# Turning the query/key chunks of an mLSTM mixer by VectorE blocks and ScalarE copies in place of TensorE transposes, with a new timetable for the mixer head

## The chip, the core and the metric

The kernel runs on one core of a Trainium2 chip. The metric is the device time of one execution in microseconds. Before the change it is 2407.74 us, the median of 3 runs (2407.58 to 2408.61).

## The reference, cut to what matters

The program computes two blocks in a row over 256 rows of width 2048, all in float32: a first block (windowed attention and a gated feed-forward layer), and a second one whose first layer is an mLSTM mixer and whose second layer attends in a band. The change is in the mixer, and there in what happens to one head:

```python
def mlstm_mixer(h, w_in, conv_w, conv_b, gate_b, g_head, w_out):
    proj = h @ w_in                       # query/key, value, o, z: 512 columns a head each
    qk = jax.nn.silu(causal_conv(proj[..., :A_V0], conv_w, conv_b))   # 4 taps over the rows
    v, o, z = proj[..., A_V0:A_O0], proj[..., A_O0:A_Z0], proj[..., A_Z0:A_G0]
    ...
    ht = mlstm_chunkwise(heads(q), heads(k), heads(v), li, lf)
    ht = rmsnorm(ht, g_head)
    y = jax.nn.sigmoid(o) * ht * jax.nn.silu(z)
    return y @ w_out

def causal_conv(u, w, b):                 # out[s] = b + sum_j w[j] * u[s - 3 + j]
    ...
```

The kernel works on a head as plain causal attention over the 256 rows: scores of queries and keys, times a decay, divided by a sum. Queries and keys come out of the projection with rows on partitions. The convolution runs over rows, so they are turned first: channels on partitions, rows along the free axis.

## The kernel before, in words

Weights come in tiles of 256x512 (a **slot**, 512 KB). ScalarE copies a tile to `WH` in fp32r (its upper part, L1563), VectorE subtracts that from the tile and leaves the rest in `WL` (L2206), and TensorE multiplies three times for each row block and each half of the tile (L1171: upper by upper, L1172: weight rest by upper, L1173: weight upper by activation rest): 12 matmuls of 512 columns per slot. There are four `WH`/`WL` buffers (`NH`), and ScalarE and VectorE stand `LOOK` = 3 slots ahead of TensorE: at the point of their programs where TensorE starts slot g, they make slot g+3, whose buffer comes free when TensorE ends slot g-1. TensorE waits at the start of each slot for both halves of its tile. VectorE also reduces streamed tiles of other weight matrices (L2187, the "modulation" tiles) woven in among the weight tiles, about one to three slots.

Eight slots with one accumulator pair are a **chunk**. A mixer head has four chunks (query/key, value, o, z); after heads 3 and 7 an output projection follows. The rest of a head's work is written as tasks (`mix`, one each for TensorE, ScalarE and VectorE) that are moved on by one step at each **tick**, and there are two ticks to a slot. `yield` ends a step, `ticks(n)` lets n ticks pass. `mix` starts when chunk 0 of its head is complete; its tick 0 comes in the first slot of chunk 1, tick 32 in the first slot of chunk 3, and the next head's tick 0 is this head's tick 64. So the tick numbers are a timetable, written by hand, and every engine's queue is fixed in that order: an instruction that waits holds up all that stands behind it on its engine, the weight tiles included.

Before the change a head goes like this. Tick 0: ScalarE (L1417) and VectorE (L1973) copy the two row blocks of the query/key chunk from PSUM to `QK`. Ticks 4 and 7: TensorE turns them, four 128x128 transposes by `four_turns` (L809) each time, into a PSUM bank. Ticks 5, 6, 8 and 9: VectorE runs one `conv` each (a TENSOR_SCALAR, L1980, and three SCALAR_TENSOR_TENSOR, L1983, each waiting for the one before). Tick 10: TensorE builds the decay (L995 to L998), ScalarE takes the sigmoid of the result (L1422) and exponentials (L1427, L1428), VectorE multiplies (L2002, queries and keys are ready, `qm`). Tick 16: scores on TensorE (L1004, L1005), their product with the decay on VectorE (L2009, `pm`). Tick 17: values copied (L1433 on ScalarE, L2014 on VectorE). Ticks 22 to 24: denominator and numerators (L1015 to L1025). Ticks 48 and 49: o, z and the numerators are multiplied (L2046 to L2051).

From tick 50 the head's product `G1` is turned in a second way, without TensorE: `blocks_T` (L1645) transposes 32x32 blocks on VectorE into `TQ`, 128x512 at a time, and `quadrants` (L1229) has ScalarE put the blocks in place, 16 small copies from `TQ` to `MT`, two per tick. Then ScalarE (L1243) and VectorE (L1660) make the two parts of the output projection's operand from `MT`. The feed-forward layer uses the same two helpers.

Of the kernel before, what the change touches and what calls it, by code (L numbers as in the profile page):

```python
# [43 lines left out]
TQ_FFN, TQ_MIX, TQ_KEYS = 0, 11, 19  # L44

MV = {k: i + 1 for i, k in enumerate("qk cva cvb qm pm vv den q2 nv0 nv1 z0 y0 z1 y1".split())}
MA = {k: i + 1 for i, k in enumerate("qk sg ee vv sn0 sn1 o0 o1 z".split())}
# [512 lines left out]
def build(nc, A, out):  # L560
    ctx = ExitStack()
    with ctx:
# [203 lines left out]
        def tensor_program(e):  # L766
# [163 lines left out]
            def gates(_):  # L930
                b, full = take("gate")
                w.wait_ge(s_gact, 1)
                w.wait_ge(s_gate, 1)
                for k in range(8):
                    w.wait_ge(s_xt, 16 + (POS[4 + k // 2] if k < 4 else POS[8 + k]))
                    for kt in (2 * k, 2 * k + 1):
                        o, a = b[0:16, 0:256], XTH[:, kt]
                        e.matmul(o, WGH[:, kt], a, start=(kt == 0), stop=False)
                        e.matmul(o, WGL[:, kt], a, start=False, stop=False)
                        i = e.matmul(o, WGH[:, kt], XTL[:, kt], start=False, stop=(kt == 15))  # L940
                    if k < 7:
                        yield from ticks(1 if k < 4 else 2)
                i.then_inc(full, 1)
                yield
                give("gate", s_gact, 2)
                yield
                b, full = take("gate_t")
                w.wait_ge(s_gact, 2)
                for t in range(2):
                    i = e.transpose(b[:, 16 * t:16 * t + 16], GS[:, 128 * t:128 * t + 128], ident[0:16, 0:16])  # L950
                i.then_inc(full, 1)
                yield
                give("gate_t", s_gate, 2)
                yield from ticks(2)
                b, full = take("gate_sum")
                w.wait_ge(s_gate, 4)
                w.wait_ge(s_nsel, 4)
                e.matmul(b[:, 0:8], Ut, glf[:, 0], start=True, stop=True)
                e.matmul(b[:, 8:16], onesf, glf[:, 0], start=True, stop=False)
                e.matmul(b[:, 8:16], Ut, glf[:, 1], start=False, stop=True).then_inc(full, 1)  # L960
                yield
                give("gate_sum", s_gate, 5)
                yield
                b, full = take("gate_c")
                w.wait_ge(s_gate, 6)
                for t in range(2):
                    i = e.transpose(b[0:8, 128 * t:128 * t + 128], gc[:, t], ident[:])
                i.then_inc(full, 1)
                give("gate_c", s_gate, 7)
                yield from ticks(4)  # L970
                b, full = take("gate_m")
                w.wait_ge(s_gate, 8)
                for t in range(2):
                    i = e.transpose(b[:, 8 * t:8 * t + 8], MM[:, 128 * t:128 * t + 128], ident[0:8, 0:8])
                i.then_inc(full, 1)
                give("gate_m", s_gate, 9)
                yield

            def mix(h, ends, free):
# [3 lines left out]
                yield from ticks(4)  # L983
                for half in range(2):
                    b, full = take(("qkT", h, half))
                    w.wait_ge(s_mixa, ata("qk"))
                    w.wait_ge(s_mix, at("qk"))
                    four_turns(b, lambda j, t: QK[:, t, 128 * (2 * half + j):128 * (2 * half + j) + 128], full)
                    yield from ticks(2)
                    give(("qkT", h, half), s_mix, at("cva" if half == 0 else "cvb"))  # L990
                    yield
# [7 lines left out]
                give(("decay", h), s_mixa, ata("ee"))  # L999
                yield from ticks(6)  # L1000
# [7 lines left out]
                yield  # L1008
                gfree[ends[1][0]] = [(s_mixa, ata("vv")), (s_mix, at("vv"))]
                yield from ticks(5)  # L1010
                b, full = take(("den", h))
                w.wait_ge(s_mix, at("vv"))
# [16 lines left out]
                yield from ticks(6)  # L1029
                gfree[ends[2][0]] = [(s_mixa, ata("o0")), (s_mixa, ata("o1"))]  # L1030
                yield from ticks(16)
# [156 lines left out]
        def scalar_program(e):  # L1188
# [209 lines left out]
            def gates(_):  # L1398
                yield from ticks(11)
                b = full("gate")  # L1400
                e.activation(GS, b[0:16, 0:256], ACT.Copy).then_inc(s_gact, 1)
                yield from ticks(2)
                w.wait_ge(s_gate, 3)
                e.activation(gt2, gt, ACT.Exp).then_inc(s_gact, 1)
                w.wait_ge(s_gact, 3)
                e.activation(gt, gt2, ACT.Ln, bias=onesf[:, 0:1]).then_inc(s_gact, 1)
                yield from ticks(9)
                w.wait_ge(s_gate, 9)
                e.activation(thr, gt2, ACT.Exp, scale=-1.0).then_inc(s_gact, 1)
                yield  # L1410

            def mix(h, ends, free):
                at = lambda k, hh=h: NMV * hh + MV[k]
                w.wait_ge(s_unit, ends[0][1])
                if h:
                    w.wait_ge(*filled(("qkT", h - 1, 1)))
                e.activation(QK[:, 0], Gb[ends[0][0]][0][:, :], ACT.Copy).then_inc(s_mixa, 1)  # L1417
                yield from ticks(10)
                w.wait_ge(s_mix, at("cvb"))
                if h:  # L1420
                    w.wait_ge(s_mix, at("y1", h - 1))
                e.activation(SG, CV.rearrange("p a b -> p (a b)"), ACT.Sigmoid).then_inc(s_mixa, 1)  # L1422
# [6 lines left out]
                yield from ticks(7)  # L1429
                w.wait_ge(s_unit, ends[1][1])  # L1430
                if h:
                    w.wait_ge(s_mix, at("y1", h - 1))
                e.activation(VV[:, 0], Gb[ends[1][0]][0][:, :], ACT.Copy).then_inc(s_mixa, 1)  # L1433
                yield from ticks(6)
# [167 lines left out]
        def vector_program(e):  # L1602
# [335 lines left out]
            def gates(_):  # L1938
# [17 lines left out]
                yield from ticks(2)  # L1956
# [9 lines left out]
            def mix(h, ends, free):  # L1966
# [23 lines left out]
                yield from ticks(5)  # L1990
# [7 lines left out]
                yield  # L1998
# [5 lines left out]
                yield from ticks(6)  # L2004
# [20 lines left out]
                yield from ticks(3)  # L2025
# [15 lines left out]
                yield from ticks(22)  # L2041
# [12 lines left out]
                w.wait_ge(s_mt, MT_MIX + h)  # L2054
# [433 lines left out]
```

## Time and profile before

| what | value |
|---|---|
| median of 3 runs | 2407.74 us |
| the profiled execution, its own time | 2407.68 us |
| its span, first to last instruction | 2405.9 us |
| TensorE matmuls busy | 2389.5 us, 99% of the span |
| VectorE busy | 1746.5 us, 73% |
| ScalarE busy | 1312.5 us, 55% |
| granted TensorE clock | 0.999 of full speed |

Busy time is the union of an engine's instructions. Matmuls are pipelined and their ends are modelled: two matmuls of the stream start 0.23 us apart while each is shown as 0.39 us long. So a pause of TensorE shorter than about 0.16 us shows only in the starts, and the starts are what is read here. Idle time is given with the instruction that ended it. "x4" in a timeline merges four instructions of one kind in a row.

### The profile page before, as it was taken

How to read it: one execution, taken by the hardware profiler on the slowest of the kernel's cores; microseconds unless marked ns; L12 is line 12 of the kernel's file. 1: busy time of each engine (PE TensorE's matmuls, PEld its weight loads, DVE VectorE, ACT ScalarE, POOL GpSimd, SP SyncE). 2: the span in 40 equal slices, each digit the busy share in tenths (PEclk: the TensorE clock that was granted, in tenths of full speed). 3: DMA queues.
4: the chain of work that ended last, by engine and by line, in shares of the span. 5: the costliest groups of instructions: out<-in, count | busy, mean ns of one | idle time of the engine just before them, and what ended most of it. 6: DMA issues, size and time to landing. Idle time of an engine off the chain costs nothing.

```text
span 2405.9 us, 30632 instructions
## 1 busy us (share of the span) xinstructions
PE 2389.5 (99%) x11049; PEld 1948.7 (81%) x11049; DVE 1746.5 (73%) x2436; ACT 1312.5 (55%) x1911; POOL 45.1 (2%) x65
## 2 busy tenths in 40 slices
PE   9999999999999999999999999999999999999998
PEld 7777888888888888778888888888888778888887
DVE  8885778677787776668778677677776676666665
ACT  6665465545553555555545544545455576655553
POOL 1100000000000000000000000000000000000000
PEclk9999999999999999999999999999999999999999
DMA  8445889788889897477777787777777457776654
GB/s 297 145 132 173 271 291 309 256 303 303 284 314 307 289 318 229 158 229 241 239 235 234 243 271 242 238 235 236 240 240 241 154 186 267 249 242 213 227 192 139
DMA packets 161831, 578.14 MB, mean 240 GB/s; under 512 B 18289, under 2 KB 20593, under 8 KB 161681
## 3 DMA queue, kind: packets, MB, share of 16 engines
q1 hardware_dynamic: 160432, 572.64, 71.4%
q0 software_dynamic: 1104, 3.28, 0.4%
q8 instruction: 90, 1.47, 0.3%
q14 instruction: 61, 0.49, 0.1%
q10 hardware_dynamic: 144, 0.26, 0.0%
HBM read 574.01 MB, written 2.10 MB: 239 GB/s over the span
## 4 chain that ended last, share of the span: by engine, by line
PE 94%; DVE 2%; ACT 2%; DMA 1%; issue 1%; POOL 0%; SPq 0%; DVEq 0%; ACTq 0%
PE PS L1171 30%; PE PS L1173 30%; PE PS L1172 30%; DVE WL L2206 1%; ACT WH L1563 1%; PE PS L914 1%; DMA X<-in_x 0%; PE PS L809 0%; PE PS L882 0%; DVE X L2173 0%; PE PS L1004 0%; PE PS L1072 0%; PE PS L1024 0%; PE PS L1025 0%; PE PS L1021 0%
## 5 line engine op out<-in xcount | busy, mean ns | idle before, releaser
L2206 DVE TENSOR_TENSOR WL<-W,WH 128x1024 fp32r<-128x1024 f32 x814 | 988.5, 1221 | 509.9 <-ACT WH L1563 503.9
L1563 ACT ACTIVATE WH<-W 128x1024 fp32r<-128x1024 f32 x814 | 855.1, 1058 | 723.6 <-PE PS L1173 681.0
L1171 PE MATMUL PS<-WH,XTH 128*128 128x512 f32 x2144 | 853.7, 398 | 2.8 <-DVE XTL L1718 1.2
L1173 PE MATMUL PS<-WH,XTL 128*128 128x512 f32 x2144 | 835.7, 390 | 0.0
L1172 PE MATMUL PS<-WL,XTH 128*128 128x512 f32 x2144 | 835.1, 389 | 0.0
L1171 PEld LDWEIGHTS PS<-WH,XTH 128*128 128x128 f32 x2144 | 402.7, 188 | 93.7 <-issue 11.4
L1173 PEld LDWEIGHTS PS<-WH,XTL 128*128 128x128 f32 x2144 | 402.5, 188 | 85.4
L1172 PEld LDWEIGHTS PS<-WL,XTH 128*128 128x128 f32 x2144 | 402.9, 188 | 83.8 <-issue 3.8
L1171 PE MATMUL PS<-WH,YTH 128*128 128x512 f32 x1120 | 440.2, 393 | 3.5 <-DVE WL L2206 2.4
L1173 PE MATMUL PS<-WH,YTL 128*128 128x512 f32 x1120 | 436.2, 389 | 0.0
L1172 PE MATMUL PS<-WL,YTH 128*128 128x512 f32 x1120 | 436.1, 389 | 0.0
L1171 PEld LDWEIGHTS PS<-WH,YTH 128*128 128x128 f32 x1120 | 210.3, 188 | 53.4 <-issue 9.0
L1173 PEld LDWEIGHTS PS<-WH,YTL 128*128 128x128 f32 x1120 | 210.3, 188 | 44.2
L1172 PEld LDWEIGHTS PS<-WL,YTH 128*128 128x128 f32 x1120 | 210.4, 188 | 42.3
L1229 ACT ACTIVATE MT<-TQ 32x256 f32<-32x256 f32 x304 | 126.3, 415 | 72.1 <-DVE TQ L1645 67.9
L2187 DVE CUSTOM_DVE_ANT_0 W<-W,acc,cols 128x1024 f32<-128x1024 f32 x96 | 122.6, 1277 | 0.8 <-ACT ZG L1551 0.8
L2187 DVE CUSTOM_DVE_ANT_0 W<-W,ZG,mods 128x1024 f32<-128x1024 f32 x96 | 122.7, 1278 | 0.0
L2241 DVE SCALAR_TENSOR_TENSOR acc<-W,SC,acc 128x512 f32<-128x512 f32 x64 | 48.1, 752 | 2.3
L1983 DVE SCALAR_TENSOR_TENSOR AR<-PS,cols,AR 128x255 f32<-128x255 f32 (+2 forms) x96 | 46.2, 482 | 3.4
L2238 DVE SCALAR_TENSOR_TENSOR acc<-W,SC,acc 128x512 f32<-128x512 f32 x56 | 41.7, 745 | 0.0
L1507 ACT ACTIVATE AR<-AR,st 128x128 f32<-128x128 f32 (+1 forms) x32 | 14.3, 449 | 44.4 <-DVE st L2110 44.4
L1645 DVE STREAM_TRANSPOSE TQ<-AR 128x512 f32<-128x512 f32 x46 | 31.6, 700 | 0.7
(286 smaller groups left out, 1192.6 us busy)
## 6 DMA issues: line engine op xcount, KB each, us to landing
W<-in_vec SPq DMA_DIRECT2D x192, 512.0 KB, 4.5
W<-in_avoz SPq DMA_DIRECT2D x192, 512.0 KB, 4.5
W<-in_wg SPq DMA_DIRECT2D x88, 512.0 KB, 5.1
W<-in_wu SPq DMA_DIRECT2D x88, 512.0 KB, 4.9
W<-in_wd SPq DMA_DIRECT2D x88, 512.0 KB, 4.9
W<-in_gate SPq DMA_DIRECT2D x64, 512.0 KB, 4.6
W<-in_aqk SPq DMA_DIRECT2D x64, 512.0 KB, 4.7
W<-in_aout SPq DMA_DIRECT2D x64, 512.0 KB, 4.4
```

The source lines that it names most:

```text
L914: i = e.matmul(b[64 * a:64 * a + 64, 0:m], V1[:, k, 64 * g:64 * g + 64], PT[P % 2][a][:, m * k:m * k + m], start=(k == 0), stop=(k == t))
L1171: e.matmul(p, x, WH[:, g % NH, j], start=first, stop=False)
L1172: e.matmul(p, x, WL[:, g % NH, j], start=False, stop=False)
L1173: i = e.matmul(p, y, WH[:, g % NH, j], start=False, stop=last)
L1229: i = e.activation(o, TQ[a].rearrange("p t (j b r) -> p t j b r", j=4, b=4)[:, :, :, b], ACT.Copy)
L1563: e.activation(WH[:, n % NH], W[:, i % NW], ACT.Copy).then_inc(s_hi, 1)
L1645: i = e.transpose(TQ[:, t], src[:, t])
L1983: i = e.scalar_tensor_tensor(out=o[:, s:256], in0=u[:, 0:256 - s], scalar=wt[3 - s], in1=o[:, s:256], op0=ALU.mult, op1=ALU.add)
L2187: e.tensor_tensor_reduce(W[:, s].rearrange("p k n -> p (k n)"), W[:, s].rearrange("p k n -> p (k n)"), SCR[h], 1.0, dst if h else cols[:, ...
L2206: e.tensor_tensor(l, src, h.bitcast(F32), ALU.subtract).then_inc(s_lo, 1)
L2238: step(e.scalar_tensor_tensor(out=a, in0=W[:, s, 0], scalar=SC[:, 2 * k:2 * k + 1], in1=a, op0=ALU.mult, op1=ALU.add))
L2241: e.scalar_tensor_tensor(out=a, in0=W[:, s, 1], scalar=SC[:, 2 * k + 1:2 * k + 2], in1=a, op0=ALU.mult, op1=ALU.add).then_inc(s_ada, 1)
```

## The change

The queries and keys of a head are now turned as `G1` is. At ticks 1 and 2 VectorE transposes the blocks of `QK` into `TQ`, at ticks 3 to 10 ScalarE copies the 16 quadrants to `MT`, and the convolutions read `MT` in SBUF at ticks 11, 12, 14 and 15. The two `four_turns` of each head leave TensorE's program, 64 transposes in all, and so do their two PSUM banks. `MT` and `TQ` are counted twice per head (`MT_MIX + 2 * h + 1` and `+ 2`). What follows is moved: values are copied at ticks 17 (ScalarE) and 18 (VectorE), the sigmoid and the exponentials come at tick 20 behind them, `qm` at tick 20, scores at tick 26, `pm` at tick 27, denominator at tick 33, numerators at 34 and 35, o at tick 37. The decay stays at TensorE's tick 10; z and the turn of `G1` stay at ticks 48 to 60. In the task `gates`, which runs beside head 0, two steps come two ticks later.

```diff
 MT_FFN, MT_MIX = 0, 11
-TQ_FFN, TQ_MIX, TQ_KEYS = 0, 11, 19
-
-MV = {k: i + 1 for i, k in enumerate("qk cva cvb qm pm vv den q2 nv0 nv1 z0 y0 z1 y1".split())}
-MA = {k: i + 1 for i, k in enumerate("qk sg ee vv sn0 sn1 o0 o1 z".split())}
+TQ_FFN, TQ_MIX, TQ_KEYS = 0, 11, 27
+
+MV = {k: i + 1 for i, k in enumerate("qk cva cvb vv qm pm den q2 nv0 nv1 z0 y0 z1 y1".split())}
+MA = {k: i + 1 for i, k in enumerate("qk vv sg ee sn0 sn1 o0 o1 z".split())}
 NMV, NMA = len(MV), len(MA)
...
     gfree[ends[0][0]] = [(s_mixa, ata("qk")), (s_mix, at("qk"))]
-    yield from ticks(4)
-    for half in range(2):
-        b, full = take(("qkT", h, half))
-        w.wait_ge(s_mixa, ata("qk"))
-        w.wait_ge(s_mix, at("qk"))
-        four_turns(b, lambda j, t: QK[:, t, 128 * (2 * half + j):128 * (2 * half + j) + 128], full)
-        yield from ticks(2)
-        give(("qkT", h, half), s_mix, at("cva" if half == 0 else "cvb"))
-        yield
+    yield from ticks(10)
     b, full = take(("decay", h))
...
     give(("decay", h), s_mixa, ata("ee"))
+    yield from ticks(10)
+    gfree[ends[1][0]] = [(s_mixa, ata("vv")), (s_mix, at("vv"))]
     yield from ticks(6)
...
     give(("qk", h), s_mix, at("pm"))
-    yield
-    gfree[ends[1][0]] = [(s_mixa, ata("vv")), (s_mix, at("vv"))]
-    yield from ticks(5)
+    yield from ticks(7)
     b, full = take(("den", h))
-    w.wait_ge(s_mix, at("vv"))
+    w.wait_ge(s_mix, at("pm"))
     w.wait_ge(s_mixa, ata("vv"))
...
     give(("num", h, 1), s_mix, at("nv1"))
-    yield from ticks(6)
+    yield
     gfree[ends[2][0]] = [(s_mixa, ata("o0")), (s_mixa, ata("o1"))]
-    yield from ticks(16)
+    yield from ticks(10)
     gfree[ends[3][0]] = [(s_mix, at("z0")), (s_mix, at("z1"))]
...
     if h:
-        w.wait_ge(*filled(("qkT", h - 1, 1)))
+        w.wait_ge(s_tq, TQ_MIX + 2 * h)
     e.activation(QK[:, 0], Gb[ends[0][0]][0][:, :], ACT.Copy).then_inc(s_mixa, 1)
-    yield from ticks(10)
-    w.wait_ge(s_mix, at("cvb"))
+    yield from ticks(3)
+    yield from quadrants(TQ_MIX + 2 * h + 1, MT, 2, s_mt)
+    yield from ticks(6)
+    w.wait_ge(s_unit, ends[1][1])
     if h:
         w.wait_ge(s_mix, at("y1", h - 1))
+    e.activation(VV[:, 0], Gb[ends[1][0]][0][:, :], ACT.Copy).then_inc(s_mixa, 1)
+    yield from ticks(3)
+    w.wait_ge(s_mix, at("cvb"))
     e.activation(SG, CV.rearrange("p a b -> p (a b)"), ACT.Sigmoid).then_inc(s_mixa, 1)
...
     e.activation(EE[:, 256:384], b[:, 256:384], ACT.Exp, bias=gc[:, 1, h:h + 1]).then_inc(s_mixa, 1)
-    yield from ticks(7)
-    w.wait_ge(s_unit, ends[1][1])
-    if h:
-        w.wait_ge(s_mix, at("y1", h - 1))
-    e.activation(VV[:, 0], Gb[ends[1][0]][0][:, :], ACT.Copy).then_inc(s_mixa, 1)
-    yield from ticks(6)
+    yield from ticks(15)
     sn = hd[:, h, 4:6]
...
         yield
-    yield from ticks(7)
     w.wait_ge(s_unit, ends[2][1])
     if h:
-        w.wait_ge(s_mt, MT_MIX + h)
+        w.wait_ge(s_tq, TQ_MIX + 2 * h)
     for t in range(2):
         e.activation(G1[:, t], Gb[ends[2][0]][t][:, :], ACT.Sigmoid).then_inc(s_mixa, 1)
-    yield from ticks(16)
+    yield from ticks(11)
     w.wait_ge(s_unit, ends[3][1])
...
     yield from ticks(5)
-    yield from quadrants(TQ_MIX + h + 1, MT, 2, s_mt)
+    yield from quadrants(TQ_MIX + 2 * h + 2, MT, 2, s_mt)
     base = CGH + 4 * h - 4 * (h % 4)
     w.wait_ge(s_unit, free)
-    yield from pairs_T(MT_MIX + h + 1, 4 * (h % 4), lambda kt: cols[:, base + kt:base + kt + 1])
+    yield from pairs_T(MT_MIX + 2 * h + 2, 4 * (h % 4), lambda kt: cols[:, base + kt:base + kt + 1])
...
     if h:
-        w.wait_ge(*filled(("qkT", h - 1, 1)))
+        w.wait_ge(s_tq, TQ_MIX + 2 * h)
     e.tensor_copy(QK[:, 1], Gb[par][1][:, :]).then_inc(s_mix, 1)
...
     def conv(half, j):
-        b = full(("qkT", h, half))
+        w.wait_ge(s_mt, MT_MIX + 2 * h + 1)
         wcol = 2 * h + j + 16 * half
-        u, o = b[:, 256 * j:256 * j + 256], CV[:, 2 * half + j]
+        u, o = MT[:, 2 * half + j], CV[:, 2 * half + j]
         wt = [cols[:, CCW + 32 * q + wcol:CCW + 32 * q + wcol + 1] for q in range(4)]
...
-    yield from ticks(5)
+    yield
+    w.wait_ge(s_mixa, ata("qk"))
+    w.wait_ge(s_mix, at("qk"))
+    yield from blocks_T(QK)
+    yield from ticks(8)
     conv(0, 0)
...
     conv(1, 1)
-    yield
+    yield from ticks(3)
+    par, g = ends[1]
+    w.wait_ge(s_unit, g)
+    e.tensor_copy(VV[:, 1], Gb[par][1][:, :]).then_inc(s_mix, 1)
+    yield from ticks(2)
     w.wait_ge(s_mixa, ata("sg"))
...
                     ALU.mult).then_inc(s_mix, 1)
-    yield from ticks(6)
+    yield from ticks(7)
     b = full(("qk", h))
...
                            op1=ALU.mult).then_inc(s_mix, 1)
-    yield
-    par, g = ends[1]
-    w.wait_ge(s_unit, g)
-    e.tensor_copy(VV[:, 1], Gb[par][1][:, :]).then_inc(s_mix, 1)
-    yield from ticks(5)
+    yield from ticks(6)
     d1, rr1, sn, q1, q2, qr = (hd[:, h, 2 * q:2 * q + 2] for q in range(6))
...
     w.wait_ge(s_mix, at("y1"))
-    w.wait_ge(s_mt, MT_MIX + h)
     yield from blocks_T(G1)
```

VectorE, head 3 (heads are counted from 0), from its copy of the query/key chunk on. Before:

```order
L1973 COPY AR<-PS 128x512
L2206 TENSOR_TENSOR WL<-W,WH 128x1024
L2187 ISA W,mods<-W,acc,cols 128x1024
L2187 ISA mods 128x1
L2206 TENSOR_TENSOR WL<-W,WH 128x1024
L1980 TENSOR_SCALAR AR<-PS,cols 128x256
L1983 SCALAR_TENSOR_TENSOR AR<-PS,cols,AR 128x255
L1983 SCALAR_TENSOR_TENSOR AR<-PS,cols,AR 128x254
L1983 SCALAR_TENSOR_TENSOR AR<-PS,cols,AR 128x253
L2206 TENSOR_TENSOR WL<-W,WH 128x1024
L1980 TENSOR_SCALAR AR<-PS,cols 128x256
```

After, the same place:

```order
L1964 COPY AR<-PS 128x512
L1636 STREAM_TRANSPOSE TQ<-AR 128x512
L2200 TENSOR_TENSOR WL<-W,WH 128x1024
L2181 ISA W,mods<-W,acc,cols 128x1024
L2181 ISA mods 128x1
L1636 STREAM_TRANSPOSE TQ<-AR 128x512
L2200 TENSOR_TENSOR WL<-W,WH 128x1024 x3
L2181 ISA W,mods<-W,ZG,mods 128x1024
L2181 ISA mods 128x1
L2200 TENSOR_TENSOR WL<-W,WH 128x1024
L1971 TENSOR_SCALAR AR<-MT,cols 128x256
L1974 SCALAR_TENSOR_TENSOR AR<-MT,cols,AR 128x255
```

Before, two weight tiles (L2206) stand between the copy and the first convolution (L1980); now five do (L2200), with the two block transposes (L1636) among them. The reductions of modulation tiles (here L2187, there L2181) keep their place among the weight tiles. The convolution's input is `MT` and no longer a PSUM bank.

ScalarE, the same head, from its last part of the previous head's operand on. Before:

```order
L1243 ACTIVATE YTH<-MT,cols 128x256 x2
L1563 ACTIVATE WH<-W 128x1024
L1243 ACTIVATE YTH<-MT,cols 128x256 x2
L1563 ACTIVATE WH<-W 128x1024
L1417 ACTIVATE AR<-PS 128x512
L1563 ACTIVATE WH<-W 128x1024 x5
```

After:

```order
L1235 ACTIVATE YTH<-MT,cols 128x256 x2
L1554 ACTIVATE WH<-W 128x1024
L1235 ACTIVATE YTH<-MT,cols 128x256 x2
L1554 ACTIVATE WH<-W 128x1024
L1409 ACTIVATE AR<-PS 128x512
L1554 ACTIVATE WH<-W 128x1024
L1221 ACTIVATE MT<-TQ 32x2x4x32 x2
L1554 ACTIVATE WH<-W 128x1024
L1221 ACTIVATE MT<-TQ 32x2x4x32 x4
L1554 ACTIVATE WH<-W 128x1024
L1221 ACTIVATE MT<-TQ 32x2x4x32 x4
```

Where five weight tiles (L1563) followed each other, small copies from `TQ` to `MT` (L1221) now stand between the tiles (L1554), up to four behind each. The sigmoid (L1422 before) is further down.

TensorE, before, where the first half of a head's query/key chunk is turned:

```order
L1173 MATMUL PS<-WH,XTL 128x512
L1171 MATMUL PS<-WH,XTH 128x512
L1172 MATMUL PS<-WL,XTH 128x512
L1173 MATMUL PS<-WH,XTL 128x512
L809 MATMUL PS<-ident,AR 128x128 x4
L1171 MATMUL PS<-WH,XTH 128x512
```

The row L809 and its twin three ticks on are gone from each head; the stream of L1171 to L1173 goes on there without a break.

## Rows read from the trace of the kernel before

**Rows 1.** The page: busy time, share and count by engine; the chain that ended last.
```profile
PE 2389.5 (99%) x11049; PEld 1948.7 (81%) x11049; DVE 1746.5 (73%) x2436; ACT 1312.5 (55%) x1911; POOL 45.1 (2%) x65
...
PE 94%; DVE 2%; ACT 2%; DMA 1%; issue 1%; POOL 0%; SPq 0%; DVEq 0%; ACTq 0%
```

**Rows 2.** Groups of TensorE: count | busy us, mean ns | idle before us, releasers.
```profile
L1171 PE MATMUL PS<-WH,XTH 128*128 128x512 f32 x2144 | 853.7, 398 | 2.8 <-DVE XTL L1718 1.2 <-DVE WL L2206 0.7 <-ACT WH L1563 0.5
```

**Rows 3.** Timeline of TensorE, 1100 to 1125 us, head 1: start, length us, engine, line.
```profile
1099.69 0.39 PE L1172 MATMUL PS<-WL,XTH 128*128 128x512 f32 x1
...
1108.76 0.40 PE L1173 MATMUL PS<-WH,XTL 128*128 128x512 f32 x1
1108.99 0.60 PE L809 MATMUL PS<-ident,AR 128*128 128x128 f32 x4
...
1113.33 0.39 PE L1173 MATMUL PS<-WH,XTL 128*128 128x512 f32 x1
```

**Rows 4.** Timeline of TensorE in head 3: first matmuls of four slots.
```profile
1289.95 0.39 PE L1171 MATMUL PS<-WH,XTH 128*128 128x512 f32 x1
...
1292.67 0.39 PE L1171 MATMUL PS<-WH,XTH 128*128 128x512 f32 x1
...
1304.52 0.39 PE L1171 MATMUL PS<-WH,XTH 128*128 128x512 f32 x1
...
1308.38 0.40 PE L1171 MATMUL PS<-WH,XTH 128*128 128x512 f32 x1
```

**Rows 5.** Timeline of VectorE, end of head 2 and start of head 3.
```profile
1276.96 1.30 DVE L1645 STREAM_TRANSPOSE TQ<-AR 128x512 f32<-128x512 f32 x2
...
1295.04 0.68 DVE L1973 COPY AR<-PS 128x512 f32<-128x512 f32 x1
1295.64 1.21 DVE L2206 TENSOR_TENSOR WL<-W,WH 128x1024 fp32r<-128x1024 f32 x1
1296.77 1.27 DVE L2187 CUSTOM_DVE_ANT_0 W<-W,acc,cols 128x1024 f32<-128x1024 f32 x1
...
1297.98 1.22 DVE L2206 TENSOR_TENSOR WL<-W,WH 128x1024 fp32r<-128x1024 f32 x1
1299.12 0.53 DVE L1980 TENSOR_SCALAR AR<-PS,cols 128x256 f32<-128x256 f32 x1
...
1310.62 1.22 DVE L2206 TENSOR_TENSOR WL<-W,WH 128x1024 fp32r<-128x1024 f32 x1
```

**Rows 6.** Timeline of ScalarE, the turn of head 2's product: first and last quadrants.
```profile
1278.29 0.85 ACT L1229 ACTIVATE MT<-TQ 32x256 f32<-32x256 f32 x2 [3.40 <-DVE TQ L1645]
...
1288.62 0.84 ACT L1229 ACTIVATE MT<-TQ 32x256 f32<-32x256 f32 x2
```

**Rows 7.** Groups of VectorE by form: conv's operations, and others like them on SBUF.
```profile
L1980 DVE TENSOR_SCALAR AR<-PS,cols 128x256 f32<-128x256 f32 x32 | 17.2, 537 | 0.0
...
L1689 DVE SCALAR_TENSOR_TENSOR XTL<-YA,cols,XTH 128x256 fp32r<-128x256 f32 x16 | 7.0, 479 | 4.8 <-ACT XTH L1257 4.6
L1689 DVE SCALAR_TENSOR_TENSOR XTL<-PS,cols,XTH 128x256 fp32r<-128x256 f32 x16 | 7.0, 479 | 13.4 <-ACT XTH L1257 13.4
...
L1733 DVE TENSOR_SCALAR AR<-GG,mods 128x256 f32<-128x256 f32 x8 | 2.9, 408 | 0.0
```

**Rows 8.** Timelines, heads 1, 2, 4: TensorE's first matmul of chunk 1, VectorE's copy.
```profile
1102.18 0.39 PE L1171 MATMUL PS<-WH,XTH 128*128 128x512 f32 x1
...
1107.89 0.68 DVE L1973 COPY AR<-PS 128x512 f32<-128x512 f32 x1
...
1196.08 0.39 PE L1171 MATMUL PS<-WH,XTH 128*128 128x512 f32 x1
...
1200.58 0.69 DVE L1973 COPY AR<-PS 128x512 f32<-128x512 f32 x1
...
1470.87 0.39 PE L1171 MATMUL PS<-WH,XTH 128*128 128x512 f32 x1
...
1473.31 0.68 DVE L1973 COPY AR<-PS 128x512 f32<-128x512 f32 x1
```

More of the change, by code:

```diff
@@ L1406, in gates @@
                 e.activation(gt, gt2, ACT.Ln, bias=onesf[:, 0:1]).then_inc(s_gact, 1)
-                yield from ticks(9)
+                yield from ticks(11)
                 w.wait_ge(s_gate, 9)
@@ L1441, in mix @@
                     yield
-                yield from ticks(7)
                 w.wait_ge(s_unit, ends[2][1])
                 if h:
-                    w.wait_ge(s_mt, MT_MIX + h)
+                    w.wait_ge(s_tq, TQ_MIX + 2 * h)
                 for t in range(2):
                     e.activation(G1[:, t], Gb[ends[2][0]][t][:, :], ACT.Sigmoid).then_inc(s_mixa, 1)
-                yield from ticks(16)
+                yield from ticks(11)
                 w.wait_ge(s_unit, ends[3][1])
@@ L1955, in gates @@
                 e.tensor_tensor(gc, gat[:, :, 0:8], gB, ALU.subtract).then_inc(s_gate, 1)
-                yield from ticks(2)
+                yield from ticks(4)
                 b = full("gate_c")
@@ L1997, in mix @@
                 conv(1, 1)
-                yield
+                yield from ticks(3)
+                par, g = ends[1]
+                w.wait_ge(s_unit, g)
+                e.tensor_copy(VV[:, 1], Gb[par][1][:, :]).then_inc(s_mix, 1)
+                yield from ticks(2)
                 w.wait_ge(s_mixa, ata("sg"))
@@ L2010, in mix @@
                                        op1=ALU.mult).then_inc(s_mix, 1)
-                yield
-                par, g = ends[1]
-                w.wait_ge(s_unit, g)
-                e.tensor_copy(VV[:, 1], Gb[par][1][:, :]).then_inc(s_mix, 1)
-                yield from ticks(5)
+                yield from ticks(6)
                 d1, rr1, sn, q1, q2, qr = (hd[:, h, 2 * q:2 * q + 2] for q in range(6))
@@ L2024, in mix @@
                 step(e.reciprocal(rr1, d1))
-                yield from ticks(3)
+                yield from ticks(4)
                 settle()
@@ L2040, in mix @@
                     e.tensor_scalar(VV[:, t], b[:, :], qr[:, t:t + 1], None, ALU.mult).then_inc(s_mix, 1)
-                yield from ticks(22)
+                yield from ticks(10)
                 par, g = ends[3]
```

## The prediction

> **What bounds the kernel now.** I read the page first: TensorE is busy for 99% of the span, and 94% of the chain that ended last is its own [rows 1]. Then its groups: before 2144 upper-by-upper matmuls it idled 2.8 us in all, 0.7 of them for weight tiles from VectorE [rows 2]. So TensorE's queue is the time, and the other engines cost nothing while they deliver in time. Then its timeline, by starts, since lengths are modelled: 40 matmuls take 1108.76 - 1099.69 = 9.07 us, 0.227 each [rows 3]. A slot of 12 is 2.72 us, from 1289.95 to 1292.67, and the slot with the decay 3.86, from 1304.52 to 1308.38 [rows 4]. Last, the timelines of VectorE and ScalarE at a head's start, since there the change puts its work [rows 5, 6].
>
> The trace's own time is 2407.68 us, its span 2405.9. The sum below is made against 2407.68, which is the median (2407.74) within 0.1.
>
> **What leaves TensorE.** Between the L1173 at 1108.76 and the one at 1113.33 lie one group of four transposes and 18 matmuls [rows 3]. The 18 alone would take 18 x 0.227 = 4.08 us, the interval is 4.57, so a group costs 0.49 (its modelled 0.60 overlaps its neighbours). Two groups in each of 8 heads: 16 x 0.49 = **7.8 us** off the queue that sets the time. Nothing is late in their place on TensorE itself. The PSUM banks only get freer. The decay stays at tick 10.
>
> Head 0 may return a little more. Its convolutions and the sigmoid with its table loads now come later, and behind slots that the gates' matmuls make longer. All waits for VectorE's tiles in that group sum to 0.7 us over the program [rows 2], so the term lies between 0 and 0.7. I take the middle, **0.4 us**.
>
> **What comes to VectorE and ScalarE.** A head adds two block transposes to VectorE; the pair took 1.30 us at the end of head 2 [rows 5], say 0.61 to the next instruction and 0.69 to its own end, as the like-sized copy is 0.68 long with the next one 0.60 behind. It adds 16 copies to ScalarE. In the turn of head 2's product the same 16, with four weight tiles between them, ran from 1278.29 to 1288.62 + 0.84, which is 11.17 us [rows 6]. That is 2.8 us per slot against TensorE's 2.72, so ScalarE catches up nothing meanwhile, and the convolutions must wait for its last copy. Whether VectorE's tiles then arrive in time decides what is left of the 7.8 us. I count from TensorE's start of chunk 1 (P = 0) and call slots from there 0, 1, 2.
>
> Head 3. P is 1289.95 [rows 4] and VectorE's copy starts at 1295.04, so at 5.09 [rows 5]. Then, by the new order: copy 0.60, transpose 0.61, weight tile 1.14 (1297.98 to 1299.12), modulation tile 1.21 (1296.77 to 1297.98), second transpose 0.69 to its end, 0.03 to ScalarE: the quadrants start at R = 9.37. ScalarE is idle until then. MT is complete at R + 11.17. The last weight tile before the first convolution (slot 8's) leaves ScalarE just ahead of the last pair of copies, at R + 10.33; VectorE needs 1.14 for it, so the first convolution starts at R + 11.5.
>
> From there the order is as before in kind: four convolutions, three weight tiles, one modulation tile. Before, they ran from 1299.12 to 1310.62, and the closing weight tile ended 1.22 later: 12.72 us [rows 5]. The source is now SBUF. A TENSOR_SCALAR of 256 elements takes 537 ns from PSUM and 408 from SBUF; a SCALAR_TENSOR_TENSOR takes 479 from either [rows 7]. So four times 0.13 goes, and 12.2 is left. That closing tile is slot 11's: ready at R + 23.7. TensorE reaches slot 11 at 10 x 2.72 + 3.86 = 31.06. It is late by R - 7.36, in head 3 by 2.0 us. Earlier tiles hold: slot 5's is ready near R + 3.2, 12.6 against 13.6, slot 10's near R + 17.6, 27 against 28.3.
>
> One place for the Trainium skill. Rows 7 show no gain for three of a convolution's four operations. Its page "VectorE: DVE Perf Modes", section "The TRN2 errata", gives VectorE a fixed 58 cycles from SBUF and 120 from PSUM; by that all four would save 65 ns (an estimate from the page), a head 1.04 us where I count 0.52, and the sum would be 2404.3. The trace disagrees: 479 and 479.
>
> The other heads by the same line. Head 1: copy at 1107.89 - 1102.18 = 5.71 [rows 8], no modulation tile between the transposes, R = 5.71 + 3.07 = 8.78, late by 1.4. Head 2: 4.50, R = 7.57, late by 0.2. Head 4 follows the output projection and starts rested, at 2.44 [rows 8]; even with 0.4 of waiting for its tile R is 5.9, 1.5 early. The modulation tiles fall alike every three heads, so heads 5, 6 and 7 are taken as 2, 3 and 1. Head 0 has longer slots, and I count none. In heads 1, 4 and 7 the modulation tile stands ahead of the first convolution; the total is the same. Together 2 x (1.4 + 0.2 + 2.0) = **7.3 us** that TensorE waits where it did not before.
>
> The other moves I cost at nothing. ScalarE's old wait for the convolutions ahead of the sigmoid, and some of its wait for the numerators, go, but it is not the bound. qm comes at tick 20 and the scores at 26, six ticks apart as before. Each of these is hidden by TensorE's stream; if a cover goes, the second rival says what it costs.
>
> **Sum.** 2407.68 - 7.8 - 0.4 + 7.3 = **2406.8 us**. If R or the convolution block is off by 0.5 us in every head, the loss is 4.8 or 10.2, since head 2's kind stops at zero on one side: 2404.3 to 2409.7.
>
> **Rivals.**
> *The cushion holds.* Nothing is late and the whole saving stands: 2407.68 - 8.2 = 2399.5. For it: VectorE is busy 73% and ScalarE 55% of the span [rows 1], and the worst head misses by only 2.0 us in 31. It needs the tiles 2 us earlier in head 3: operations on MT at double speed throughout, or an R that I have too late. Against it: rows 7, and the turn in rows 6, which shows ScalarE's rate with no slack. If only half of those 2 us appear the loss is about 2.8 us and the time 2402.3, already nearer to this rival.
> *The wait moves to the scores.* TensorE's scores at tick 26 wait for qm, and in head 1 VectorE has, behind slot 11's tile, two modulation tiles (2 x 1.21), two weight tiles (2 x 1.14), the value copy (0.60) and the product itself (a tile's length, 1.2): ready at R + 30.2 = 39.0. TensorE comes to them in the second half of slot 13, at 31.06 + 1.4 + 2 x 2.72 + 1.36 = 39.3. One microsecond more in that queue would show in heads 1 and 7 beside the 7.3: 2408.2.
> *Slower: the head start is longer still.* Place: the quadrant copies and the convolutions of each head. Price: every microsecond by which slot 11's tile comes later than R + 23.7 costs six heads one each. With 1.4 us (copies of 0.50 us for 0.42, or each convolution 0.35 longer) the loss is 15.7 and the time 2407.68 - 8.2 + 15.7 = 2415.2. It passes "no change" from 0.95 us more per head. For it: ScalarE's 16 copies read TQ while VectorE runs weight and modulation tiles, and both queues are full there. Against it: rows 6 were taken beside the same kind of work.
> *The page's fixed term:* 2404.3, as worked above for every convolution operation.
>
> **Chances.** Forecast 0.55, cushion 0.27, page's term 0.05, scores 0.05, slower 0.08. A measurement of this kernel can tell about 0.2%, 4.8 us, from no change. Faster than that: the cushion's 0.27 and 0.05 from halfway cases, 0.32. Slower: 0.08 and 0.04 from the forecast's upper tail, 0.12. No change 0.56. The range goes from the cushion's 2399.5 to 2411, past the forecast's own 2404.3 to 2409.7.
>
> **What would show it.** TensorE's timeline: no group of four transposes at a head's start; 0.49 us less in each of two slots. VectorE's: block transposes right behind the copy; the first convolution's TENSOR_SCALAR near 0.41 us, its other three near 0.48; in head 3 the first convolution about 20.9 us after chunk 1 begins. ScalarE's: an idle time of about 4 us ended by TQ at the head's start, then 11.2 us of copies and tiles. TensorE's groups: idle time of about 7 us ended by WL, in pieces of 1.4, 0.2 and 2.0 us at slot 11, none in heads 0 and 4. If the idle time by WL stays under 3 us, the walk through VectorE's queue is wrong. If it is over 12, the copies or the convolutions are longer than their rows.

## The result, and the profile after

The changed kernel takes 2416.04 us (median of 6 runs, 2415.14 to 2417.21) against 2407.66 before (6 runs, 2407.53 to 2408.61): the ratio is 1.0035, 95% interval 1.0025 to 1.0045. It is slower by 8.4 us. I had forecast 2406.8, no change, with a range up to 2411. The profiled execution took 2415.3 us with a span of 2413.5, 7.6 more than before.

The page of the changed kernel, to be read against [rows 1, 2]:

```profile
PE 2385.8 (99%) x10985; PEld 1944.8 (81%) x10985; DVE 1752.7 (73%) x2452; ACT 1367.6 (57%) x2039; POOL 45.1 (2%) x65
...
PE 87%; DVE 6%; ACT 4%; issue 3%; DMA 1%; POOL 0%; SPq 0%; DVEq 0%; ACTq 0%
...
L1163 PE MATMUL PS<-WH,XTH 128*128 128x512 f32 x2144 | 853.4, 398 | 10.8 <-DVE WL L2200 8.9
```

TensorE has 64 matmuls fewer, and its idle time ahead of the upper-by-upper matmuls (L1163, L1171 before) went from 2.8 to 10.8 us, 8.9 of them for VectorE's weight tiles (L2200, L2206 before). The shares of VectorE and ScalarE in the chain that ended last went from 2% each to 6% and 4%. So the mechanism that I had worked out is there. Where it bites, in head 3 (slots counted as before, chunk 1 begins at 1293.74), VectorE first, the rows that answer to [rows 5]:

```profile
1298.83 0.68 DVE L1964 COPY AR<-PS 128x512 f32<-128x512 f32 x1
1299.62 0.71 DVE L1636 STREAM_TRANSPOSE TQ<-AR 128x512 f32<-128x512 f32 x1
1300.25 1.18 DVE L2200 TENSOR_TENSOR WL<-W,WH 128x1024 fp32r<-128x1024 f32 x1
1301.36 1.28 DVE L2181 CUSTOM_DVE_ANT_0 W<-W,acc,cols 128x1024 f32<-128x1024 f32 x1
...
1302.56 0.71 DVE L1636 STREAM_TRANSPOSE TQ<-AR 128x512 f32<-128x512 f32 x1
...
1314.77 0.41 DVE L1971 TENSOR_SCALAR AR<-MT,cols 128x256 f32<-128x256 f32 x1
...
1325.78 2.35 DVE L2200 TENSOR_TENSOR WL<-W,WH 128x1024 fp32r<-128x1024 f32 x2
```

ScalarE, first and last pair of its copies, as in [rows 6]:

```profile
1303.30 0.85 ACT L1221 ACTIVATE MT<-TQ 32x256 f32<-32x256 f32 x2 [4.98 <-DVE TQ L1636]
...
1313.62 0.84 ACT L1221 ACTIVATE MT<-TQ 32x256 f32<-32x256 f32 x2
```

And TensorE at slot 11:

```profile
1324.60 0.39 PE L1165 MATMUL PS<-WH,XTL 128*128 128x512 f32 x1
1327.14 0.56 PE L1163 MATMUL PS<-WH,XTH 128*128 128x512 f32 x1 [2.16 <-DVE WL L2200]
1327.50 0.63 PE L1164 MATMUL PS<-WL,XTH 128*128 128x512 f32 x1
1327.93 0.63 PE L1165 MATMUL PS<-WH,XTL 128*128 128x512 f32 x1
...
1330.86 0.39 PE L1163 MATMUL PS<-WH,XTH 128*128 128x512 f32 x1
1331.09 0.40 PE L1164 MATMUL PS<-WL,XTH 128*128 128x512 f32 x1
```

The quadrants start at R = 9.56 (I had 9.37), the first convolution 11.47 later (11.5), the closing weight tile starts at 1325.78, and slot 11 begins at 1327.14 where 1324.60 + 0.23 was due: 2.3 us late (2.0). What I had not seen is in the last rows: behind that pause the matmuls start 0.43 us apart and not 0.23, until 1330.9. The windows of TensorE there show why (us, then busy time and count for TensorE, its weight loads, VectorE, ScalarE and GpSimd, the granted clock, the DMA engines' share, GB/s):

```profile
1325.00:1327.00 2.00, 0.00 (x0) 0.00 (x0) 1.96 (x4) 1.09 (x2) 0.00 (x0) 1.00 0.32 129
1327.00:1328.60 1.60, 1.46 (x4) 1.20 (x5) 1.60 (x2) 1.59 (x2) 0.00 (x0) 0.62 0.37 64
1328.60:1330.20 1.60, 1.60 (x5) 1.21 (x5) 1.60 (x3) 1.34 (x3) 0.00 (x0) 0.50 1.08 294
```

The granted clock is 0.50 there, the lower of its two levels (1.2 GHz), after TensorE had stood still for 2 us. The second thing that I had not seen is in head 0, on TensorE and VectorE:

```profile
1022.38 0.39 PE L1165 MATMUL PS<-WH,XTL 128*128 128x512 f32 x1
1025.71 0.69 PE L987 MATMUL PS<-AR 8*128 8x256 f32 x2 [2.94 <-DVE AR L1951]
```
```profile
1022.19 1.23 DVE L2200 TENSOR_TENSOR WL<-W,WH 128x1024 fp32r<-128x1024 f32 x1 [1.57 <-ACT WH L1554]
...
1024.98 0.68 DVE L1951 TENSOR_TENSOR_SCAN AR<-AR 8x256 f32<-8x256 f32 x1
```

The decay (L987) waits for the gates' running maximum (L1951), which stands in VectorE's queue behind weight tiles, which wait for ScalarE, which is copying quadrants between its tiles.

From the starts, head by head (chunk 1 of a head to chunk 1 of the next; the last to the end), the changed kernel against the one before: head 0 +3.3 us, 1 +0.9, 2 -0.3, 3 +3.1, 4 -1.0, 5 -0.3, 6 +1.2, 7 +0.8. That is 7.6, all of the difference in span; outside the mixer nothing moved.

### The profile page after: what moved, and what is told of

The parts are those of the page before. It is cut to its first block, busy times and chain, and to the rows that moved or that the text cites. A ratio compares the mean times of both kernels' runs of the same rounds, so it can differ in the third digit from the quotient of the medians.

```text
span 2413.5 us, 30640 instructions
## 1 busy us (share of the span) xinstructions
PE 2385.8 (99%) x10985; PEld 1944.8 (81%) x10985; DVE 1752.7 (73%) x2452; ACT 1367.6 (57%) x2039; POOL 45.1 (2%) x65
## 3 DMA queue, kind: packets, MB, share of 16 engines
q8 instruction: 89, 1.46, 0.3%
## 4 chain that ended last, share of the span: by engine, by line
PE 87%; DVE 6%; ACT 4%; issue 3%; DMA 1%; POOL 0%; SPq 0%; DVEq 0%; ACTq 0%
PE PS L1163 28%; PE PS L1165 27%; PE PS L1164 27%; DVE WL L2200 2%; ACT MT L1221 2%; ACT WH L1554 1%; DVE AR L1974 1%; DVE W L2181 1%; PE PS L914 1%; DMA X<-in_x 0%; PE PS L882 0%; DVE X L2167 0%; PE PS L1064 0%; PE PS L998 0%; PE PS L1016 0%
## 5 line engine op out<-in xcount | busy, mean ns | idle before, releaser
L2200 DVE TENSOR_TENSOR WL<-W,WH 128x1024 fp32r<-128x1024 f32 x814 | 988.8, 1221 | 513.9 <-ACT WH L1554 507.3
L1554 ACT ACTIVATE WH<-W 128x1024 fp32r<-128x1024 f32 x814 | 856.3, 1058 | 684.1 <-PE PS L1165 642.8
L1163 PE MATMUL PS<-WH,XTH 128*128 128x512 f32 x2144 | 853.4, 398 | 10.8 <-DVE WL L2200 8.9
L1163 PEld LDWEIGHTS PS<-WH,XTH 128*128 128x128 f32 x2144 | 403.3, 188 | 103.5 <-issue 18.7
L1163 PE MATMUL PS<-WH,YTH 128*128 128x512 f32 x1120 | 440.2, 393 | 3.5 <-DVE WL L2200 2.5
L1163 PEld LDWEIGHTS PS<-WH,YTH 128*128 128x128 f32 x1120 | 210.2, 188 | 53.4 <-issue 9.0
L1221 ACT ACTIVATE MT<-TQ 32x256 f32<-32x256 f32 x432 | 179.5, 415 | 105.8 <-DVE TQ L1636 99.7
L2181 DVE CUSTOM_DVE_ANT_0 W<-W,acc,cols 128x1024 f32<-128x1024 f32 x96 | 122.7, 1278 | 0.8 <-ACT ZG L1542 0.8
L2181 DVE CUSTOM_DVE_ANT_0 W<-W,ZG,mods 128x1024 f32<-128x1024 f32 x96 | 122.7, 1278 | 0.0
L1974 DVE SCALAR_TENSOR_TENSOR AR<-MT,cols,AR 128x255 f32<-128x255 f32 (+2 forms) x96 | 46.4, 483 | 3.4
L1636 DVE STREAM_TRANSPOSE TQ<-AR 128x512 f32<-128x512 f32 x62 | 42.9, 702 | 1.4
```

What stands on the lines that cost most here:

```text
L1163: e.matmul(p, x, WH[:, g % NH, j], start=first, stop=False)
L1221: i = e.activation(o, TQ[a].rearrange("p t (j b r) -> p t j b r", j=4, b=4)[:, :, :, b], ACT.Copy)
L1554: e.activation(WH[:, n % NH], W[:, i % NW], ACT.Copy).then_inc(s_hi, 1)
L1636: i = e.transpose(TQ[:, t], src[:, t])
L1974: i = e.scalar_tensor_tensor(out=o[:, s:256], in0=u[:, 0:256 - s], scalar=wt[3 - s], in1=o[:, s:256], op0=ALU.mult, op1=ALU.add)
L2181: e.tensor_tensor_reduce(W[:, s].rearrange("p k n -> p (k n)"), W[:, s].rearrange("p k n -> p (k n)"), SCR[h], 1.0, dst if h else cols[:, ...
```

## The experiments

Each ran five rounds beside the kernel before. "R" and the slots are those of the prediction. The theory after the result: the turn saves 7.8 us on TensorE and costs it about 17 (16.4 by the traces) through its place in two fixed queues, in three ways: slot 11's tile late in six heads, the decay of head 0, and the low clock behind long pauses. Rivals: the new timetable is what costs, or the added work as such (ScalarE's pace, memory bandwidth).

**The timetable alone.** TensorE turns the chunks again, and the copies on ScalarE (`quadrants`) and the block transposes on VectorE (`blocks_T`) go; all other tick numbers are as changed. "..." stands for lines left out:

```diff
-                yield from ticks(10)
+                yield from ticks(4)
+                for half in range(2):
+                    b, full = take(("qkT", h, half))
+                    ...
+                    four_turns(b, ..., full)
+                    yield from ticks(3)
                 b, full = take(("decay", h))
...
-                yield from quadrants(TQ_MIX + 2 * h + 1, MT, 2, s_mt)
...
-                yield from blocks_T(QK)
```

> The new timetable alone: queries and keys are turned by TensorE again (four transposes at ticks 4 and 7 of each head), the convolutions read PSUM at their new ticks 11, 12, 14 and 15, values ahead of the sigmoid. Theory: the changed kernel (2416.0) loses 17 us through the turn's place in the queues (slot 11's tile late in six heads, the decay of head 0 behind the gates' scan, a low granted clock after the two longest pauses), so here all of it goes and the 7.8 us of transposes come back: 2407 (2406 to 2408), TensorE's idle time before weight matmuls as before, under 7 us. Rival: the timetable itself (later scores, value copies, sigmoid) makes TensorE wait: 2412 or more.

Measured: 2406.42 us (2406.13 to 2406.9), ratio 0.9995 (0.9986 to 1.0004). The timetable costs nothing; head 0 alone is 1.2 us shorter than before, the other heads the same to 0.05. The gates' scan stands two ticks later here too, and TensorE does not wait for it. The rival falls. Its page shows next to no waits:

```profile
L1173 PE MATMUL PS<-WH,XTH 128*128 128x512 f32 x2144 | 853.3, 398 | 3.4 <-DVE XTL L1717 1.2 <-DVE WL L2217 1.2 <-ACT WH L1562 0.5
```

**The decay later.** From here on the changed kernel is the base:

```diff
                 give("gate_c", s_gate, 7)
-                yield from ticks(4)
+                yield from ticks(8)
...
-                yield from ticks(10)
+                yield from ticks(16)
                 b, full = take(("decay", h))
```

> The changed kernel with TensorE's decay at tick 16 instead of 10 and the gates' last transposes, addition and exponential four ticks later. Theory: only head 0 changes: 3.0 us of idle time ahead of its decay and about 1.9 us of slow matmuls behind it go, 2411.1 (2410 to 2412); the waits at slot 11 stay at 1.8, 0.5, 2.3, 0.5, 2.1 and 1.7 us. Rival (head 0's time is lost to the added copies and transposes wherever the decay stands): 2415 to 2417.

Measured: 2410.91 us (2409.25 to 2411.47), ratio 1.0012 (1.0003 to 1.0021). Head 0 went from 100.2 to 96.0 us, the other heads stayed within 0.1. The added copies are still in head 0, so it was the order that cost there.

**Convolutions spread.** One weight tile behind each:

```diff
                 conv(0, 0)
-                yield
+                yield from ticks(2)
                 conv(0, 1)
                 yield from ticks(2)
                 conv(1, 0)
-                yield
+                yield from ticks(2)
                 conv(1, 1)
-                yield from ticks(3)
+                yield
```

> The changed kernel with the four convolutions at ticks 11, 13, 15 and 17, so that one weight tile follows each. Theory: slot 11's tile has three convolutions ahead of it and not four, so it is ready 1.88 us earlier, at R + 21.8, late by 0.5 us at most in head 3 and by 0.2 in head 6; the other 8.3 us of waiting, the 0.5 of restarts and the 1.7 of low clock in head 3 go: 2405.6 (2404.5 to 2407). Head 0 keeps its 3 us at the decay. Rival (the engines are short of time in that stretch as a whole, so that the wait only moves to slot 12 or 13): 2412 or more.

Measured: 2408.38 us (2408.03 to 2409.91), ratio 1.0004 (0.9995 to 1.0013). Between the two. Slot 11 is in time in heads 1, 2, 5 and 7, and the slow stretch in head 3 is gone. But slot 12 is now late in heads 1 and 7:

```profile
1138.57 0.39 PE L1165 MATMUL PS<-WH,XTL 128*128 128x512 f32 x1
1140.12 0.47 PE L1163 MATMUL PS<-WH,XTH 128*128 128x512 f32 x1 [1.17 <-DVE WL L2200]
```

I had counted slot 12's tile with one modulation tile ahead of it; in heads 1 and 7 there are two. There the wait moved by one slot, as the rival said, and most of it stayed: 1.33 and 1.30 us late, where slot 11 had been 1.77 and 1.72. Heads 3 and 6 are still late by 0.7 and 0.4 us over slots 11 and 12.

**Both block transposes together**, ahead of the weight tile:

```diff
-                yield from blocks_T(QK)
-                yield from ticks(8)
+                for t in range(2):
+                    i = e.transpose(TQ[:, t], QK[:, t])
+                i.then_inc(s_tq, 1)
+                yield from ticks(10)
```

> The changed kernel with both block transposes of a head in VectorE's tick 1, ahead of the weight tile and of the modulation tile that stood between them. Theory: R comes 1.14 us earlier in heads 1, 2, 5 and 7 and 2.35 in heads 0, 3 and 6, and slot 11's wait shrinks by just that: 0.6, 0, 0, 0, 0 and 0.6 us are left in heads 1, 2, 3, 5, 6 and 7. In head 0 the wait for the scan shrinks to about 1 us and its slow matmuls go. Sum 2402 (2400.5 to 2404). Rival (ScalarE's copies set the pace and the start does not matter): 2414 to 2417.

Measured: 2402.13 us (2401.3 to 2403.15), ratio 0.9977 (0.9968 to 0.9987). One tick earlier for one instruction of 0.7 us is worth 13.9 us. In head 1 the late start of slot 11 is down to 0.64 us (1.77 in the changed kernel), in heads 2, 3, 5 and 6 it is gone. ScalarE's copies start 1.13 us earlier in head 1 and 2.34 in head 3, as expected. Head 1:

```profile
1133.57 0.39 PE L1165 MATMUL PS<-WH,XTL 128*128 128x512 f32 x1
1134.43 0.47 PE L1163 MATMUL PS<-WH,XTH 128*128 128x512 f32 x1 [0.47 <-DVE WL L2202]
```

One part of the expectation failed, although the sum came out: in head 0 the wait for the scan did shrink, to 1.30 us, but the slow matmuls behind it did not go. Head 0 takes 97.6 us here and 94.8 with the decay later as well (the run with two mends below), so 2.8 us of the loss were still in it, 1.3 of them the pause and about 1.4 the lower clock. TensorE ahead of the decay, and the windows over it (the granted clock is the number ahead of the last two):

```profile
1022.96 0.69 PE L987 MATMUL PS<-AR 8*128 8x256 f32 x2 [1.30 <-DVE AR L1951]
```
```profile
1022.00:1026.00 4.00, 3.04 (x12) 2.10 (x12) 3.76 (x7) 1.02 (x3) 0.00 (x0) 0.82 0.88 272
1026.00:1030.00 4.00, 4.00 (x15) 3.16 (x15) 2.55 (x5) 2.56 (x3) 0.00 (x0) 0.75 0.41 129
```

**The start later.** The opposite test; the second block transpose is done twice:

```diff
-                yield from blocks_T(QK)
+                e.transpose(TQ[:, 0], QK[:, 0])
+                yield
+                step(e.transpose(TQ[:, 1], QK[:, 1]))
+                settle()
+                e.transpose(TQ[:, 1], QK[:, 1]).then_inc(s_tq, 1)
+                yield
```

> The changed kernel with the second block transpose of each query/key chunk done twice, so that ScalarE starts about 0.8 us later in each head; the result of the second is the same. Theory: every microsecond of a later start costs TensorE one in each of heads 0, 1, 2, 3, 5, 6 and 7, so 5.6 us, and the longer pauses (2.5 to 3.1 us in heads 1, 3, 6, 7) are now all followed by matmuls at the lower granted clock, 1.7 us each where the changed kernel showed it in head 3 alone: 2421.6 from the starts alone, up to 2427 with the clock. Rival (ScalarE's copies set the pace, or VectorE has slack): 2416 to 2418.

Measured: 2424.91 us (2423.73 to 2425.61), ratio 1.0072 (1.0058 to 1.0085). Against the changed kernel's trace every head but 4 is 0.7 to 0.8 us longer, 5.3 in all, and heads 1 and 6 a further 1.6 each, for now they too have slow matmuls; 8.5 in all. Head 4, with 1.5 us to spare, does not move. The price is one for one, as said. The clock is less regular than I said, for not all of the longer pauses were followed by the lower level: TensorE paused 1.93 us in head 1 and 1.90 in head 7, and only the first was followed by the lower level. Head 1 and head 7, in windows ahead of the first matmul and behind it:

```profile
1138.00:1140.50 2.50, 0.74 (x3) 0.67 (x4) 2.50 (x3) 1.97 (x2) 0.00 (x0) 1.00 0.02 7
1140.50:1143.50 3.00, 3.00 (x9) 2.30 (x8) 3.00 (x5) 2.05 (x4) 0.00 (x0) 0.52 0.90 235
...
1798.00:1800.50 2.50, 0.60 (x4) 0.20 (x2) 2.43 (x5) 1.24 (x2) 0.00 (x0) 1.00 0.11 44
1800.50:1803.50 3.00, 3.00 (x13) 2.51 (x14) 3.00 (x5) 2.78 (x4) 0.00 (x0) 1.00 0.66 198
```

**Matmuls in the pause.** Is it the pause that lowers the clock? Twelve matmuls of ones fill the pause of head 0 (they write the decay's bank, which the decay then overwrites):

```diff
                 b, full = take(("decay", h))
+                for _ in range(12 if h == 0 else 0):
+                    e.matmul(b[:, :]..., ones[:], ones[:]..., start=True, stop=True)
                 w.wait_ge(s_gate, 8)
```

> The changed kernel with 12 matmuls of ones ahead of the decay of head 0, which write the decay's own bank and are overwritten; they stand in TensorE's pause of 3.3 us before the gates' scan and take 2.7 of it. Theory: the slow matmuls behind that pause come from the pause; without it the granted clock stays at its upper level and the 1.9 us go, 2414.1 against 2416.0, with the decay starting at the same time. Rival (the matmuls are slow because VectorE and ScalarE take memory bandwidth at that moment): 2416 or above.

Measured: 2413.51 us (2412.01 to 2414.19), ratio 1.0023 (1.0014 to 1.0032), 2.5 less than the changed kernel for 2.9 us more work. The trace:

```profile
1022.68 2.88 PE L986 MATMUL PS<-ones 128*128 128x512 f32 x12
1025.77 0.69 PE L990 MATMUL PS<-AR 8*128 8x256 f32 x2 [0.20 <-DVE AR L1954]
```

The decay starts at the same time (1025.77 and 1025.71), and what follows runs at the full level. Here the window from 1026 us on, then the same one of the changed kernel:

```profile
1026.00:1030.00 4.00, 4.00 (x20) 2.99 (x20) 3.13 (x6) 1.59 (x2) 0.00 (x0) 1.00 0.85 247
```
```profile
1026.00:1030.00 4.00, 4.00 (x15) 2.81 (x14) 2.54 (x5) 0.70 (x1) 0.00 (x0) 0.62 0.84 251
```

20 instructions instead of 15 in four microseconds, with the same memory traffic and more beside it on both other engines. Head 0 is 1.4 us shorter. So in head 0 the pause is the cause and bandwidth is not. The pause's length alone does not say whether the clock falls: the 1.30 us of head 0 with both block transposes together were followed by the lower level, the 1.94 us in head 6 of the changed kernel were not. The medians differ by more than that, since single runs of both kernels differ by whether head 3's or another head's pause also ends in the lower level: the eleven runs here lie at 2412.0 to 2412.3 (four) and 2413.3 to 2414.2 (seven). That last step is my reading of the times, as these runs have no trace of their own; the granted clock of the whole run, 0.999 in the four and 0.998 or 0.999 in the seven, fits it but is too coarse to show it.

**Two and three mends together.** First the transposes together with the later decay, both edits as above:

```diff
-                yield from blocks_T(QK)
-                yield from ticks(8)
+                for t in range(2):
+                    i = e.transpose(TQ[:, t], QK[:, t])
+                i.then_inc(s_tq, 1)
+                yield from ticks(10)
...
-                yield from ticks(10)
+                yield from ticks(16)
                 b, full = take(("decay", h))
```

> Both block transposes in tick 1 and the decay with the gates' end later, the convolutions at the changed kernel's ticks 11, 12, 14 and 15. Theory: of the waits only 0.6 us at slot 11 in heads 1 and 7 is left, and their restarts of 0.1: 2406.42 (timetable alone) less 7.8 of transposes plus 1.4 gives 2400.0 (2399 to 2401). Rival: the two mends overlap and give less than 2402.1.

Measured: 2400.36 us (2400.02 to 2401.44), ratio 0.9970 (0.9959 to 0.9982). Then the spread convolutions as well:

```diff
                 conv(0, 0)
-                yield
+                yield from ticks(2)
                 conv(0, 1)
```

> Three mends of the changed kernel together: both block transposes in tick 1, convolutions at ticks 11, 13, 15 and 17, the decay at tick 16 with the gates' end four ticks later. Theory: with the convolutions spread, slot 12 was late by 1.4 us in heads 1 and 7 and by about 0.5 and 0.3 at slots 11 and 12 in heads 3 and 6; a start earlier by 1.14 and 2.35 us leaves 0.2 in heads 1 and 7 and nothing else, and head 0 has no wait. So the transposes' 7.8 us and the 1.2 us that head 0 gained by the timetable alone stay saved: 2399.2 (2398 to 2400.5). Rival (some of the waits are made up again elsewhere in the head): 2402 or more.

Measured: 2399.27 us (2399.23 to 2399.43), ratio 0.9965 (0.9953 to 0.9978). This beats both kernels, by 8.3 us and 16.8. What is left of the waits, to be read against the 8.9 of the changed kernel:

```profile
L1163 PE MATMUL PS<-WH,XTH 128*128 128x512 f32 x2144 | 852.2, 397 | 2.6 <-DVE XTL L1709 1.2 <-DVE WL L2202 0.7 <-ACT WH L1554 0.5
```

## Why the prediction was wrong

*What left TensorE: right.* I had 7.8 us in all. Head 4, which never waits, takes 92.91 us instead of 93.87, so 0.96 a head and 7.7 in all. The timetable alone against all three mends gives 7.15, with 0.5 of small waits left in the latter.

*Head 0 returns something: undersized.* I took 0.4 from a bound of 0.7. The timetable alone gave 1.2. The bound was wrong, since it took only the idle time ahead of L1171 [rows 2]. In head 0 before, TensorE also waited ahead of L967 and of L1004 (0.25 and 0.23 us recorded), and recorded idle time leaves out what the modelled matmul lengths cover: by starts these two and one late slot make 1.0 us, and with the timetable alone all three are gone. The last 0.2 I can't place.

*Late tiles at slot 11: the right step, 7.3 us where 9.0 were measured* (starts late by 1.8, 0.5, 2.3, 0, 0.5, 2.1 and 1.7 us in heads 1 to 7, where I had 1.4, 0.2, 2.0, 0, 0.2, 2.0 and 1.4). The block of convolutions came out to 0.1. R was short by 0.2: the transpose starts 0.79 us behind the copy, not 0.60, for it waits for the copy's result, where the copy's old successor, a weight tile, did not. Another 0.1 lies between the tile and the matmul. Each restart then costs 0.1 more, 0.5 in all.

*"Each of these is hidden", "the decay stays at tick 10": this is the step that failed.* I walked VectorE's queue for heads 1 to 7, where slots 5 to 11 wait for weight tiles. For head 0 I wrote "I count none", and did not walk the gates' scan, which had moved by two ticks (with the timetable alone this cost nothing) and stood behind the same held-up tiles. Head 0 was to gain 1.4 us and lost 3.3. Of the 5.5 between what the transposes and the timetable save there (2.2) and that loss, 3.0 are the wait at the decay, 1.4 the slow matmuls behind it (the filled pause gives back 1.4), 0.8 an idle time at L967 a slot and a half earlier, for another step of the gates.

*The clock: not among my rivals.* 1.7 us in head 3 and the 1.4 in head 0. I priced a pause at its length. The trace before had no pause that long: its longest is 1.46 us, and its granted clock is below 1.00 only in the last 5 us.

The sum by measured terms: -7.7 - 1.2 + 9.0 + 0.5 + 5.2 + 1.7 = +7.5, of 7.6. My error of 8.5 us against the profiled run (2415.3) is 1.7 at slot 11, 0.5 of restarts, 1.7 of clock there, and 4.6 in head 0.

*The slower rival* had the right price for a head and the wrong place. Its figure, 2415.2 us, comes near the measured one (2416.0, the profiled execution 2415.3) by luck: it is made of 15.7 us of waits at slot 11, where 9.0 were measured, and leaves out head 0 and the clock. That "every microsecond" later "costs six heads one each" held in both directions: with the start 0.75 us later each of the six lost 0.7 to 0.8, the clock aside, and head 0 as well; with the start 1.13 us earlier head 1 gained 1.1. I had looked for its cause in slower copies or convolutions. The copies took 11.16 us in head 3 (1303.30 to 1314.46), as in [rows 6], and the convolutions ran as before or as in their row; the first line is from before, the others from after:

```profile
L1983 DVE SCALAR_TENSOR_TENSOR AR<-PS,cols,AR 128x255 f32<-128x255 f32 x32 | 15.4, 483 | 1.1
...
L1974 DVE SCALAR_TENSOR_TENSOR AR<-MT,cols,AR 128x255 f32<-128x255 f32 x32 | 15.5, 484 | 1.1
...
L1971 DVE TENSOR_SCALAR AR<-MT,cols 128x256 f32<-128x256 f32 x32 | 13.1, 408 | 0.0
```

That is 484 ns from SBUF for the 483 of the same operation from PSUM, and 408 for 537 [rows 7]. So the Trainium skill's fixed term ("VectorE: DVE Perf Modes", "The TRN2 errata") is not borne out here either. Its rule that an operand in PSUM holds float32 to the single rate ("Why PSUM operands drop a tier") agrees with 537 against 408 for the TENSOR_SCALAR.

*The cushion* did not hold, but it was near: one instruction moved ahead by one tick brings most of it back.

## What to carry to other kernels

Where engines run fixed queues a few tiles ahead of the bound one, walk the queue at every place where an instruction moves behind a new wait, the odd first iteration above all, and ask of each instruction there who waits for it. A short instruction that starts a long chain on another engine belongs ahead of the bulk work in its queue. A pause of the matmul engine may cost nearly twice its length (1.30 us cost about 1.4 more in one trace, 2.16 us 1.7 more in another), so one of that size is worth splitting or filling.

## What the runs showed of the hardware

Some pauses of TensorE were followed by 3 to 4 us at the lower clock level and others were not. In the ten traces all eight pauses of 2.15 to 2.94 us were, among them 2.16 in head 3 and 2.94 in head 0 of the changed kernel. Of the 23 of 1.30 to 1.96 us only two were: 1.30 us in head 0 with both block transposes together, and 1.93 in head 1 with the start later. In that last trace 1.90 us in head 7 was not, nor was 1.94 in head 6 of the changed kernel. What decides in the shorter ones is not shown. Such a stretch cost 1.4 to 1.7 us, and matmuls within the pause averted it in the one trace where they were tried. The spread of single runs was 2.1 us for the changed kernel and 0.2 for the one with all three mends; that the clock makes this difference fits the trace of each but is not shown.
